# The down projection's remainder tiles: 16 of 88 formed by accumulating transfers instead of by VectorE

## What is computed

```
h = rms_norm(x, ln2)
u = h @ w_ffn_in                      # 2048 x 11264
a, b = split(u, 2)                    # 5632 columns each
a = causal_depthwise_conv(a, conv_w, conv_b)
x = x + (gelu(a) * b) @ w_ffn_out     # 5632 x 2048: the down projection
return rms_norm(x, ln_f)
```

## Time and profile before

| | us |
|---|---|
| median of 3 runs | 1134.22 |
| the runs | 1134.22, 1134.22, 1137.91 |
| the profiled execution, time | 1137.75 |
| the profiled execution, span from first to last instruction | 1136.0 |
| busy: TensorE, VectorE, ScalarE, GpSimd | 1117.5, 699.1, 552.9, 76.2 |
| mean granted TensorE clock | 0.994 |

### The profile page before, as it was taken

The page is one execution under the profiler, slowest core; times in us unless marked ns, Lnnn a source line. Parts: engine busy times, 40 slices in busy tenths (PEclk is TensorE's granted clock), DMA queues, the critical chain, the costliest instruction groups (busy, mean ns, idle before and its releaser), DMA issues.

```text
span 1136.0 us, 16731 instructions
## 1 busy us (share of the span) xinstructions
PE 1117.5 (98%) x5730; PEld 951.3 (84%) x5730; DVE 699.1 (62%) x1010; ACT 552.9 (49%) x760; POOL 76.2 (7%) x87
## 2 busy tenths in 40 slices
PE   8999999999999999999999999999999899999996
PEld 6888888888888888888888888888888788888885
DVE  4655666666656575656666657656566555575555
ACT  5544444444445445544545545445445454554443
POOL 2000111111100001101101001011011000000001
PEclk9999999999999999999999999999999899999998
DMA  9765555554556666666666666666665556556641
GB/s 337 239 189 172 149 153 154 154 149 148 149 177 178 186 182 188 187 191 191 186 185 186 187 189 193 186 185 187 187 190 193 183 196 195 188 186 203 196 135 74
DMA packets 146240, 206.80 MB, mean 182 GB/s; under 512 B 7539, under 2 KB 75537, under 8 KB 145952
## 3 DMA queue, kind: packets, MB, share of 16 engines
q1 hardware_dynamic: 145632, 204.67, 60.0%
q0 software_dynamic: 544, 1.72, 0.4%
q10 hardware_dynamic: 32, 0.01, 0.0%
HBM read 204.17 MB, written 2.10 MB: 182 GB/s over the span
## 4 chain that ended last, share of the span: by engine, by line
PE 97%; DVE 1%; DMA 1%; ACT 0%; SPq 0%; issue 0%; DVEq 0%; ACTq 0%
PE acc L630 14%; PE acc L415 13%; PE acc L417 13%; PE acc L416 13%; PE acc L636 7%; PE bank_tr L630 7%; PE bank_s L630 7%; PE bank_tr L636 4%; PE bank_s L636 4%; PE bank_s L415 2%; PE bank_s L417 2%; PE bank_s L416 2%; PE bank_tr L417 2%; PE bank_tr L416 2%; PE bank_tr L415 2%; DMA raw<-in_w_in 1%
## 5 line engine op out<-in xcount | busy, mean ns | idle before, releaser
L961 DVE TENSOR_TENSOR w_lo<-raw,w_hi 128x1024 fp32r<-128x1024 f32 x380 | 465.6, 1226 | 403.0 <-ACT w_hi L724 401.0
L724 ACT ACTIVATE w_hi<-raw 128x1024 fp32r<-128x1024 f32 x380 | 403.0, 1061 | 564.5 <-PE acc L417 189.0
L630 PE MATMUL acc<-h_both,w_hi 128*128 128x512 f32 x704 | 220.3, 394 | 0.0
L415 PE MATMUL acc<-w_hi,h_both 128*128 128x512 f32 (+1 forms) x352 | 140.9, 400 | 1.5 <-DVE h_both L968 1.5
L636 PE MATMUL acc<-h_both,w_lo 128*128 128x256 f32 x704 | 140.6, 282 | 0.0
L417 PE MATMUL acc<-w_hi,h_both 128*128 128x512 f32 (+1 forms) x352 | 134.9, 383 | 0.0
L416 PE MATMUL acc<-w_lo,h_both 128*128 128x512 f32 (+1 forms) x352 | 134.8, 383 | 0.0
L630 PEld LDWEIGHTS acc<-h_both,w_hi 128*128 128x128 f32 x704 | 121.1, 190 | 15.1
L636 PEld LDWEIGHTS acc<-h_both,w_lo 128*128 128x128 f32 x704 | 121.0, 190 | 13.7
L630 PE MATMUL bank_s<-h_both,w_hi 128*128 128x512 f32 x352 | 109.0, 391 | 0.0
L630 PE MATMUL bank_tr<-h_both,w_hi 128*128 128x512 f32 x352 | 109.0, 390 | 0.0
(11 more groups left out here) (171 smaller groups left out, 1365.6 us busy)
## 6 DMA issues: line engine op xcount, KB each, us to landing
raw<-in_w_ffn_in SPq DMA_DIRECT2D x176, 512.0 KB, 3.6
raw<-in_w_ffn_out SPq DMA_DIRECT2D x88, 512.0 KB, 3.7
raw<-in_w_in SPq DMA_DIRECT2D x128, 256.0 KB, 3.0
raw<-in_w_out SPq DMA_DIRECT2D x32, 512.0 KB, 3.8
raw<-in_w_in SPq DMA_DIRECT2D x20, 512.0 KB, 8.6
x_res<-in_x SPq DMA_DIRECT2D x4, 512.0 KB, 10.3
decay<-table_decay POOLq DMA_DIRECT2D x1, 1024.0 KB, 9.7
lnf_row<-in_ln_f SPq DMA_DIRECT2D x1, 1024.0 KB, 6.7
```

The source lines that it names most:

```text
L415: mm(out, lhs_hi, rhs_hi, start=first, stop=False, skip_group_check=True)
L630: mm(out, w_hi[:, slot, q * COLS + ft * P:q * COLS + (ft + 1) * P], h_both[:, 2 * k + q, :, :].rearrange("p a n -> p (a n)"), start=k == 0 ...
L724: run(w_hi[:, n % SPLIT, :], raw[:, n % RAW, :], ACT.Copy).then_inc(hi_ready, 1)
L961: tt(w_lo[:, n % SPLIT, :], raw[:, n % RAW, :], w_hi[:, n % SPLIT, :].bitcast(F32), ALU.subtract).then_inc(lo_ready, 1)
```

## The change

Of the 88 tiles, 16 get their remainder in another way: those with m % 4 == 3 for m from 8 to 39 and from 48 to 79, that is 11, 15, ..., 39 and 51, 55, ..., 79. For these ScalarE makes a second copy with the scale -1 after the rounded one, into the `w_lo` slot: the rounded tile with its sign turned. VectorE leaves the tile out. GpSimd waits for that copy (`neg_ready`) and issues a transfer from `raw` to `w_lo` that adds to what is there: -hi + raw. TensorE waits for its landing (`acc_landed`) ahead of such a tile, and SP for the same landing before it loads the raw slot anew. The counts of `lo_ready` are lowered by the tiles left out. The loops of this stage become written-out code on SP, TensorE, ScalarE and VectorE, because the tiles differ now.

```diff
+def by_dma(m):
+
+    return m % 4 == 3 and (8 <= m < 40 or 48 <= m < 80)
+
+
+def by_dma_count(m):
+
+    return sum(by_dma(k) for k in range(m + 1))
...
             def free_raw(n):
 
-                if not isinstance(n, int) or n >= RAW:
+                if not isinstance(n, int):
                     sp.wait_ge(lo_ready, n - RAW + 1)
+                elif n >= RAW:
+                    sp.wait_ge(lo_ready, n - RAW + 1 - by_dma_count(n - RAW - DOWN_TILE))
+                if isinstance(n, int) and by_dma(n - RAW - DOWN_TILE):
+                    sp.wait_ge(acc_landed, 16 * by_dma_count(n - RAW - DOWN_TILE))
...
-            with sp.Fori(0, 3) as i:
-                for j in range(8):
-                    n = DOWN_TILE + 16 + j
-                    load_down(i * 8 + n, n % RAW, i * 8 + (16 + j), 0)
-            for m in range(40, 48):
-                load_down_static(m)
...
+            for m in range(16, 88):
                 load_down_static(m)
...
             def down_tile(n, pairs, m, banks, first=False, last=False):
 
-                pe.wait_ge(lo_ready, n + 1)
+                pe.wait_ge(lo_ready, n + 1 - by_dma_count(m))
+                if by_dma(m):
+                    pe.wait_ge(acc_landed, 16 * by_dma_count(m))
...
-            with pe.Fori(0, 4) as i:
-                for j in range(8):
-                    down_tile(i * 8 + (DOWN_TILE + 8 + j), i * 4 + (4 + j // 2 + 1), 8 + j, a_banks)
-            for m in range(40, 44):
+            for m in range(8, 44):
                 down_tile(DOWN_TILE + m, m // 2 + 1, m, a_banks, False, m == 43)
...
                 run(w_hi[:, n % SPLIT, :], raw[:, n % RAW, :], ACT.Copy).then_inc(hi_ready, 1)
+                if isinstance(n, int) and by_dma(n - DOWN_TILE):
+                    run(w_lo[:, n % SPLIT, :], raw[:, n % RAW, :], ACT.Copy, scale=-1.0).then_inc(neg_ready, 1)
...
                 dve.wait_ge(hi_ready, turn * tiles + (n + 1))
+                if by_dma(n - DOWN_TILE):
+                    return
                 tt(w_lo[:, n % SPLIT, :], raw[:, n % RAW, :], w_hi[:, n % SPLIT, :].bitcast(F32),
                    ALU.subtract).then_inc(lo_ready, 1)
...
             with pool.Fori(0, GROUPS - 1) as f:
                 scale_gate(f + 1)
+            for m in range(2 * FFT):
+                if by_dma(m):
+                    n = DOWN_TILE + m
+                    pool.wait_ge(neg_ready, by_dma_count(m))
+                    pool.dma_start(w_lo[:, n % SPLIT, :], raw[:, n % RAW, :].bitcast(F32R),
+                                   accum_op=ALU.add).then_inc(acc_landed, 16)
```

More of the change, by code:

```diff
@@ L207, in build @@
         a_banks, b_banks = (acc0, bank_s), (acc1, bank_tr)
+        neg_ready = sem("neg_ready")
+        acc_landed = sem("acc_landed")
         raw_landed = [sem(f"raw_landed{r}") for r in range(RAW)]
@@ L388, in _ @@
             sp.dma_start(lnf_row[:], ln_f.partition_broadcast(P)).then_inc(lnf_landed, 16)
-            with sp.Fori(0, 3) as i:
-                for j in range(8):
-                    n = DOWN_TILE + 16 + j
-                    load_down(i * 8 + n, n % RAW, i * 8 + (16 + j), 0)
-            for m in range(40, 48):
-                load_down_static(m)
-            with sp.Fori(0, 4) as i:
-                for j in range(8):
-                    n = DOWN_TILE + 48 + j
-                    load_down(i * 8 + n, n % RAW, i * 8 + (4 + j), 1)
-            for m in range(80, 88):
+            for m in range(16, 88):
                 load_down_static(m)
@@ L693, in _ @@
                 down_tile(DOWN_TILE + m, m // 2 + 1, m, b_banks, m == 44)
[L694 to L697, removed]
+            for m in range(48, 84):
                 down_tile(DOWN_TILE + m, m // 2 + 1, m, b_banks)
@@ L701, in _ @@
                 if c == 0:
-                    pe.wait_ge(lo_ready, DOWN_TILE + m + 1)
+                    pe.wait_ge(lo_ready, DOWN_TILE + m + 1 - by_dma_count(m))
                     pe.wait_ge(g_lo_ready, m // 2 + 1)
@@ L925, in _ @@
                 down_step(m, 0, m + 4)
[L926 to L929, removed]
+            for m in range(8, 48):
                 down_step(m, 0, (m + 4) % FFT)
```

## The result

The changed kernel takes 1145.13 us (median), against 1134.22 before: ratio 1.0074, 95% interval 1.0053 to 1.0096. Its three runs took 1141.52, 1145.13 and 3926.52 us; why the last took so long is not known, no other run of this study showed it, and the ratio leaves it out, so that it is smaller than the quotient of the two medians. Measured again beside the last experiments the change takes 1142.95 against 1135.71: 1.0068, 1.0054 to 1.0082. So it is slower by some 8 us, as forecast in sign, but not by the 20.5 us of the sum.

A forecast was written before the change was run, and what follows sets the result against it. TensorE, busy 98% of the span, was taken to bound the kernel. Sixteen stalls of 1.2 us (19.2) plus 1.3 for tile 51 gave 20.5, and 1134.2 + 20.5 = 1155 us, range 1135 to 1205.

The forecast's parts named there:

- parts 1, 2 and 3 of the change: Part 1: 16 subtractions off VectorE, 0 gained; part 2: negated copies fit on ScalarE, 0; part 3: loops written out, 0.
- The room of 5.6 us: Down projection, tile 11: from the transfer's issue at 910.7 to the landing needed by 916.3, 5.6 us.
- tile 51: Its rounded copy starts 1.31 us late behind four sums of squares, so it stalls another 1.3 us.
- The landing, 6.7 us: GpSimd's accumulating 512 KB transfer takes 6.7 us from issue to landing: 4.2 fixed plus 2.5 of movement.
- The movement of 2.5 us: Accumulating transfer reads both sources through the same 16 engines one behind the other: 2.5 us, against 1.27 for one pass.
- The fixed part of 4.2: Fixed part of a transfer on GpSimd's queue, taken from an 8 KB row: 4.2 us.
- the wait among loads: SP's next load waits for the landing, so engines are mostly free during the transfer: nothing added.
- the equal stall of 1.2 us: TensorE waits 1.2 us at each of the 16 tiles, 6.7 + 0.1 - 5.6; together 19.2 us.
- Part 5, SP's waits: SP's loads wait for landings with 7.6 us to spare, also with three loads in a heap: 0 lost.
- The clock: Rival, chance 0.17: TensorE stalls lower the granted clock, from landings of 7.2 to 8.7 us on, 2.8 us more each.
- the forecast's own branch (1141 to 1170): TensorE stalls of 0.4 to 2.1 us per tile, time 1141 to 1170 us, chance 0.60.
- hidden anyway: Rival, chance 0.17: transfer lands within about 5.7 us, 15 tiles wait 0 to 0.3 us, time 1134 to 1140 us.

The follow-up runs named there:

- e1: Kernel before with the down projection's loops written out, VectorE still subtracting all 88 tiles: 1134.37 us, ratio 1.0004 to the kernel before.
- e5: The change with SP's load that waits for a landing moved two places back on its queue: 1137.76 us, ratio 1.0022 to the kernel before.
- e6: The change with the 16 transfers copying instead of adding: 1136.55 us, ratio 1.0003 to the kernel before.
- e10: Kernel before with written-out loops, plus 16 loads of 8 KB on GpSimd's queue, one behind each tile's rounded copy: 1134.21 us (one execution).
- e7: The change with GpSimd, not SP, waiting for each landing and loading the freed raw slot: 1136.28 us, ratio 1.0014 to the kernel before.
- e2: The change with the negated copy ahead of the rounded one, so transfers issue about 1 us earlier: 1148.34 us, ratio 1.0127 to the kernel before.
- e4: The change with the loops of 8 tiles put back on TensorE, ScalarE and VectorE: 1142.16 us, ratio 1.0061 to the kernel before.
- e8: The change with both e5's reordered loads and e4's loops: 1136.64 us, ratio 1.0016 to the kernel before.
- e9: The change with both e5's reordered loads and e2's earlier negated copy: 1136.17 us, ratio 1.0014 to the kernel before.

## Why the prediction was right or wrong

**What bounds the kernel, parts 1, 2 and 3 of the change.** Right: TensorE's own spacing is unchanged, the 16 subtractions gave nothing, ScalarE's second copy fits, straight code alone costs nothing (e1). What part 3 left out is that code fetches can hold a landing up: alone this costs little (e5), on top of the heap it makes the largest stalls (4.4 of 6.0 us in the change).

**The room of 5.6 us, and tile 51.** Right, to a tenth (tile 63 above), with some luck: GpSimd issued 2.31 us behind the start of tile 11's rounding copy (908.32 - 906.01) and not 2.1, and a landing may come until 0.13 us ahead of the tile's first matmul (1060.13 behind 1052.81 + 7.19) and not 0.3; the two cancel. Tile 51 stalled at a quiet landing of 4.4, by 0.3 us and not 1.3 more than the others, because its landing was short.

**The landing, 6.7 us: the step that failed, in two terms of opposite sign.** The movement of 2.5 us was right (2.65; one pass 1.42 in e6). The fixed part of 4.2 was taken from the 8 KB row, which lay in a start with full queues; it is 1.8 us (4.4 - 2.65 in the quiet transfers, and the least of e10): 2.4 too much. That the start was busy stood in the text, as a rival's reason, and should have decided the value. And the wait among loads was set to nothing, because the engines would be mostly free; it was 1.1 us in the median (5.5 against 4.4) and, with a code fetch on top, up to 2.8. With both right the sum is 1.8 + 2.65 + 1.1 = 5.5 us, and 5.5 + 0.1 - 5.6 leaves no stall in 16 equal tiles: the equal stall of 1.2 us was wrong as well. What stalls TensorE is the excess of some landings over 5.5, and a sum with one landing for all cannot give the 6.0 us.

Both rules of the Trainium skill that the forecast named fit. DMA: Bandwidth & Descriptors of the Trainium skill, "Anatomy of one DMA", gives about 2.0 us and bytes over 436 GB/s, an estimate of 4.4 us with two reads. The quiet landings here take 4.4, as 1.8 + 2.65 and not 2.0 + 2.4; for the copy the estimate is 3.2, and 2.8 was measured. Collectives: The Full Stack of the Trainium skill, "The bandwidth ceiling", says that a reduction is slower for its two source reads and not for the adding. Here 2.65 us per engine stand against 1.42, which agrees, though no run shows the second read itself. The forecast set the first rule against a row that measured something else.

**Part 5, SP's waits.** "0, also with three loads in a heap" was wrong in the place it looked at: the loads were not late for their own tiles, but the heap stood in the way of the next transfer (e5 and e7). It may be that a late landing lets the heap go late, which makes the next one late: the first six tiles lost nothing and all from tile 35 on something, and from 39 on, but for tile 51, the loads in the table are 0.75 MB or more. That is read from the table and from the cure in e5 alone; how a single late landing hands on its lateness was not tried by itself.

**The clock.** Behind stalls it was not lost in the change's profiled executions: idle gaps of 1.56 us at most, granted clock 1.00 in the stretch. In e2 and e4 gaps of 1.85 to 1.89 us were followed by 0.50, where 1.74 (e2) was not, so that rival is real; in e4 it took landings of 7.6 us, inside the 7.2 to 8.7 that the forecast gave. Its price, 2.8 us in the forecast, was 1.7 in e2. The lower of the forecast's two gaps was a misreading: the earlier trace rows has 1.00 behind the gap of 1.66 us, but the trace's record of the clock begins only at 15.8 us, and the spacing of TensorE's matmuls, 0.21 us until then and 0.12 after, shows the lower level:

```profile
15.30 0.41 PE L415 MATMUL acc<-w_hi,h_both 128*128 128x256 f32 x1
15.51 0.41 PE L416 MATMUL acc<-w_lo,h_both 128*128 128x256 f32 x1
...
15.89 0.28 PE L415 MATMUL acc<-w_hi,h_both 128*128 128x256 f32 x1
16.01 0.28 PE L416 MATMUL acc<-w_lo,h_both 128*128 128x256 f32 x1
```

So that gap said nothing of what a gap leaves of the clock.

**The chances.** Slower was right; of the mechanisms, the forecast's (TensorE waits for the landing) is the one at work, with stalls a third as large. That the time, 1145.13, lies in the forecast's own branch (1141 to 1170) is partly luck: the rival *hidden anyway* had the quiet landing right and its reason too (the 8 KB row was taken in a busy start), and what made the change slower is the heap, which the forecast had put at 0.

## What to carry to other kernels

Price a transfer's fixed part from a row in a quiet stretch, and what it waits for among other transfers from the stage that it will run in; one row that holds both gives neither. When a queue's wait is moved to a later event, look not only at whether what is behind it still comes in time, but at what all of it, let loose at once, will run into. Price an accumulating transfer at twice the movement of a copy: here 4.4 us in quiet for 512 KB against 2.8. And where room is only just enough, look for rare additions such as code fetches: they made the largest stalls.

The cured forms (e5, e7, e8, e9) bring the change to about 0.2% or less above the kernel before, and none beats it: TensorE had no gap in this stage to give back.

## What the runs showed of the hardware

An accumulating transfer of 512 KB on GpSimd's queue takes each of the 16 engines 2.65 us against 1.42 for a copy, and its issue on GpSimd 0.86 against 0.53 us. A landing waits for the slowest of the 16 engines: in the longest one the last 1.9 us moved one packet of 4 KB at a time. Idle gaps of TensorE of 1.85 and 1.89 us in a full stream were followed by the granted clock of 0.50, gaps of up to 1.74 us were not. And an 8 KB load on that queue, with nothing waiting ahead of it on its own queue, took from 1.8 to 4.9 us in one and the same stage.
